# Eight small changes of order in a one-core kernel that runs two transformer blocks: first load, statistics of x, a bank, a rounding step, folds, and the last store

## Time and profile before

| | |
|---|---|
| median of 3 runs | 1286.98 us (1286.67 to 1288.11) |
| the profiled execution | 1287.98 us, its span 1286.2 us |
| TensorE busy | 1246.5 us, 97% |
| weight loads | 1096.5 us, 85% |
| VectorE | 852.2 us, 66% |
| ScalarE | 581.1 us, 45% |
| GpSimd | 101.8 us, 8% |
| transfers | 219.27 MB, 170 GB/s over the span |

### The profile page before, as it was taken

One profiled execution on the slowest core, in us unless ns is written; L12 is line 12 of the kernel. 1 busy time (PEld: TensorE's weight loads), 2 busy tenths in 40 slices (PEclk: granted clock), 3 DMA queues, 4 the chain that ended last, 5 costly groups with the idle time before them and its releaser, 6 DMA issues.

```text
span 1286.2 us, 19279 instructions
## 1 busy us (share of the span) xinstructions
PE 1246.5 (97%) x7697; PEld 1096.5 (85%) x7697; DVE 852.2 (66%) x1327; ACT 581.1 (45%) x926; POOL 101.8 (8%) x101
## 2 busy tenths in 40 slices
PE   6999999999899999999999999999999999999997
PEld 6987999987788888887787798888788997999986
DVE  5885888796697777753424884357886676555544
ACT  7655545444632222222324662246445745544533
POOL 2030001100000000000100400001330000000000
PEclk9999999999999999999999999999999999999999
DMA  8444577775376578863342363334223554555562
GB/s 329 148 140 144 194 246 248 232 243 173 132 223 194 193 233 292 290 221 111 99 137 76 121 183 99 98 99 132 83 85 112 182 180 131 187 185 186 181 196 82
DMA packets 59465, 219.27 MB, mean 170 GB/s; under 512 B 6685, under 2 KB 6721, under 8 KB 58609
## 3 DMA queue, kind: packets, MB, share of 16 engines
q1 hardware_dynamic: 56736, 205.55, 49.7%
q0 software_dynamic: 2352, 11.76, 2.6%
q10 hardware_dynamic: 288, 0.75, 0.2%
HBM read 216.95 MB, written 1.07 MB: 170 GB/s over the span
## 4 chain that ended last, share of the span: by engine, by line
PE 84%; DVE 7%; ACT 5%; issue 2%; DMA 1%; POOL 0%; DVEq 0%; SPq 0%; ACTq 0%; POOLq 0%
PE ps L2088 18%; PE ps L2090 18%; PE ps L2089 18%; PE ps L2136 3%; PE ps L2138 3%; PE ps L2137 3%; PE ps L2147 3%; PE ps L2149 3%; PE ps L2148 3%; ACT hi L693 2%; DVE lo L1291 2%; PE ps L2124 1%; PE ps L2125 1%; PE ps L2126 1%; PE ps L2616 1%
## 5 line engine op out<-in xcount | busy, mean ns | idle before, releaser
L1291 DVE TENSOR_TENSOR lo<-raw,hi 128x1024 fp32r<-128x1024 f32 x315 | 390.6, 1241 | 297.0 <-ACT hi L693 296.7
L2088 PE MATMUL ps<-nh,hi 128*128 128x256 f32 (+1 forms) x1776 | 552.7, 311 | 5.5 <-DVE lo L1291 3.3
L2089 PE MATMUL ps<-nh,lo 128*128 128x256 f32 (+1 forms) x1776 | 545.0, 307 | 0.0
L2090 PE MATMUL ps<-nl,hi 128*128 128x256 f32 (+1 forms) x1776 | 544.9, 307 | 0.0
L693 ACT ACTIVATE hi<-raw 128x1024 fp32r<-128x1024 f32 x315 | 332.3, 1056 | 437.8 <-PE ps L2090 246.7
L2088 PEld LDWEIGHTS ps<-nh,hi 128*128 128x128 f32 x1776 | 340.0, 191 | 36.1 <-issue 15.8
L2089 PEld LDWEIGHTS ps<-nh,lo 128*128 128x128 f32 x1776 | 340.1, 191 | 16.4 <-issue 1.0
L2090 PEld LDWEIGHTS ps<-nl,hi 128*128 128x128 f32 x1776 | 339.9, 191 | 15.2
L707 ACT ACTIVATE sg<-ps 128x256 f32<-128x256 f32 (+1 forms) x66 | 30.1, 455 | 132.8 <-PE ps L2090 132.8
L1278 DVE SCALAR_TENSOR_TENSOR raw<-raw,cvec 128x1024 f32<-128x1024 f32 x72 | 86.8, 1222 | 1.4
L2136 PE MATMUL ps<-hi,H 128*128 128x512 f32 x176 | 70.1, 398 | 4.2 <-DVE lo L1291 3.6
(11 more groups left out here) (372 smaller groups left out, 1316.2 us busy)
## 6 DMA issues: line engine op xcount, KB each, us to landing
raw<-in_up SPq DMA_DIRECT2D x132, 512.0 KB, 3.8
raw<-in_in SPq DMA_DIRECT2D x86, 512.0 KB, 3.6
raw<-in_w_ada SPq DMA_DIRECT2D x72, 512.0 KB, 4.5
raw<-in_down SPq DMA_DIRECT2D x66, 512.0 KB, 3.7
raw<-in_out SPq DMA_DIRECT2D x8, 512.0 KB, 4.0
raw<-in_hy_out SPq DMA_DIRECT2D x8, 512.0 KB, 3.9
raw<-in_da_out SPq DMA_DIRECT2D x8, 512.0 KB, 3.9
raw<-in_o SPq DMA_DIRECT2D x8, 512.0 KB, 3.6
```

Of the source, the lines that this page charges most:

```text
L1291: dve.tensor_tensor(lo[:, h, 0:w], raw[:, r, 0:w], hi[:, h, 0:w].bitcast(F32), ALU.subtract).then_inc(lo_done, 1)
L2088: mm(o, hi[:, h, wk], x_hi, start=first, stop=False)
L2089: mm(o, lo[:, h, wk], x_hi, start=False, stop=False)
L2090: return mm(o, hi[:, h, wk], x_lo, start=False, stop=last)
```

## The change

1. **First load:** at the start only `par[:, 0:8]` is loaded. The other 595 columns and `con` are issued by ScalarE's queue after `nh` of k = 3. Whoever uses the rest of `par` first waits for it (`par_landed` 32).
2. **Sums of x** on TensorE after slab 2 instead of slab 1.
3. **xdt** before `seg` 8 to 11 on VectorE.
4. **A turn's bank:** `turn_values(1)` uses bank 4 and waits for `o1_lo` 1 (VectorE has read bank 4) instead of `pool_lo` 2; `turn_values(2)` waits for `pool_lo` 2.
5. **Rounding** of context column k at slab k + 11 instead of k + 10 on ScalarE.
6. **Folds** wait until TensorE is through the first slab of `k2`.
7. **rows2:** row 3 is added after the first diagonal.
8. **Last store:** the last 512 columns are added and stored in two halves of 256; the last store is issued by ScalarE.

```diff
-    "x": dict(final1=4, post2=8, rows2=4, rows3=4),
+    "x": dict(final1=4, post2=8, rows2=4, rows3=5),
+VALUES_IN = (5, 4, 5)
+OUT_PARTS = ((0, 0, 512), (0, 512, 512), (1, 0, 512), (1, 512, 256), (1, 768, 256))
-            for b in range(4):
-                tt, w = b // 2, slice(b % 2 * 512, b % 2 * 512 + 512)
+            for b, (tt, at, n) in enumerate(OUT_PARTS[:-1]):
+                w = slice(at, at + n)
                 sp.wait_ge(sem("x"), since("x", "rows3") + b + 1)
                 sp.dma_start(out[:, tt, w], xtok[:, tt, w]).then_inc(sem("out_landed"), 16)
-            sp.wait_ge(sem("out_landed"), 64)
+            sp.wait_ge(sem("out_landed"), 80)
+            pool.wait_ge(slab_used, st["k2"][0].s + 1)
             pool.wait_ge(sem("kf_copied"), 6)
-            act.dma_start(par[:, :], d["params"]).then_inc(sem("par_landed"), 16)
-            act.dma_start(con[:, :], d["consts"]).then_inc(sem("con_landed"), 16)
+            act.dma_start(par[:, 0:KD], d["params"][:, 0:KD]).then_inc(sem("par_landed"), 16)
...
                 if k == 3:
+                    act.dma_start(par[:, KD:NPAR], d["params"][:, KD:NPAR]).then_inc(sem("par_landed"), 16)
+                    act.dma_start(con[:, :], d["consts"]).then_inc(sem("con_landed"), 16)
...
             act.wait_ge(sem("con_landed"), 16)
+            act.wait_ge(sem("par_landed"), 32)
             prime(0, ACT.Sqrt)
...
-                               ps[:, 5, 0:256].rearrange("p (a n) -> p a n", a=2), ACT.Copy)\
+                               ps[:, VALUES_IN[t], 0:256].rearrange("p (a n) -> p a n", a=2), ACT.Copy)\
...
-                if 10 <= x.j < 18:
-                    rounded("pre2c", xgc, x.j - 10, c_)
+                if 11 <= x.j < 19:
+                    rounded("pre2c", xgc, x.j - 11, c_)
...
+            tt, at, n = OUT_PARTS[-1]
+            act.wait_ge(sem("x"), since("x", "rows3") + len(OUT_PARTS))
+            act.dma_start(out[:, tt, at:at + n], xtok[:, tt, at:at + n]).then_inc(sem("out_landed"), 16)
...
             after(1)
+            dve.wait_ge(sem("par_landed"), 32)
...
                 if p == 10:
-                    segments(8, 12)
                     dve.wait_ge(sem("ssd_made"), 1)
...
+                    segments(8, 12)
                 if p == 11:
...
-            added_row("rows2", 3, 1, free[3])
             row_inverse("rows2", 2, ROOT + 2, INV + 2)
             diagonal("rows2", 3, 0, INV + 2)
+            added_row("rows2", 3, 1, free[3])
...
-                for b in (2 * tt, 2 * tt + 1):
+                for b in (2 * tt, 2 * tt + 1)[:2 - tt]:
                     added_row("rows3", b, 4 + tt, free[b])
+            for at in (512, 768):
+                w = slice(at, at + 256)
+                dve.wait_ge(bank_free[3], free[3])
+                dve.scalar_tensor_tensor(xr[:, 1, w], yg[:, 1, w], small[:, INV + 5:INV + 6], xr[:, 1, w],
+                                         ALU.mult, ALU.add).then_inc(sem("x"), 1)
...
-                    o = pe.transpose(ps[:, 5, tt * P:tt * P + P],
+                    o = pe.transpose(ps[:, VALUES_IN[t], tt * P:tt * P + P],
...
-                if p == 1:
+                if p == 2:
                     gathered("mix1", rinv[:, :], SUM1)
...
                 if p == 20:
-                    pe.wait_ge(sem("pool_lo"), 2)
+                    pe.wait_ge(sem("o1_lo"), 1)
                     turn_values(1)
...
-            pe.wait_ge(sem("vtok_copied"), 2)
+            pe.wait_ge(sem("pool_lo"), 2)
             turn_values(2)
```

## The result

The changed kernel takes 1278.44 us (median of 4 runs, 1278.41 to 1278.81), the kernel before beside it 1286.83 (1286.16 to 1288.11): ratio 0.9923, 95% interval 0.991 to 0.9937. That is 8.4 us faster where 14.7 were forecast, and 2 us above the top of the range. The profiled execution took 1278.81 us, its span 1277.0, where the one before took 1287.98 and 1286.2; the sum is checked against these two, a difference of 9.2.

The account below looks back on a forecast made before the run. The prediction took TensorE to bound the kernel, busy 97% of the span, with pauses and clock falls to gain. Its terms summed to -14.7 from 1287.98 us, less 1.0 for the median: 1272.3 us, range 1269.5 to 1276.5.

Parts of the forecast that it names:

- First load: At the start: fewer bytes ahead of x and slab 0 bring the first product earlier, later `con` costs nothing; -0.9 us.
- Sums of x: Early slabs: slab 2 fills the 2.56 us pause, but most returns as pauses, some 2 us before slab 6; -0.8 us.
- xdt: TensorE's 1.2 us wait for `xdt` ends, but its next products wait for `xw`; -0.4 us.
- A turn's bank: At the turn of V: the 2.71 us pause and its low clock go, slab 21 waits some 0.4; -3.5 us.
- Rounding: In `down1`: roundings leave ScalarE's circle and follow 2.72 apart, not 3.15; the 2.2 us pause goes; -5.4 us.
- Folds: In `mixed`: GpSimd's folds slow VectorE's splits; moved into `k2` they cost TensorE nothing; -3.2 us.
- rows2: Row 3's addition, 0.74 us, no longer stands before the first diagonal; -0.2 us.
- Last store: At the end: half the bytes in the last store and a shorter VectorE addition before it; -0.3 us.
- rival 1: Clock falls in a pause the change makes before slab 6, or stays low at the turn: +1.3 us; chance 0.16.
- Rival 4: At the start: first load gives nothing because issues or a late `con` eat it: +1.8 us; chance 0.06.
- rival 2: Folds aren't the cause in `mixed`, or cost as much in `k2`: +3.2 us; chance 0.07.
- Rival 5: TensorE, without its rests, gets a lower mean clock; at 0.98 the time is 1297.2 us; chance 0.02.

Follow-up runs that it names:

- con_wait_later: Changed kernel with TensorE's wait for `con` moved from behind slab 0 to ahead of the sums of x, after slab 2: 1274.92 us.
- sums_as_before: Changed kernel with the sums of x after slab 1 again, first load still split: 1275.56 us.
- filled_pause: con_wait_later with 16 more products of no use on TensorE after slab 5, in the pause before slab 6: 1273.72 us.
- wait_and_sums_at_1: Changed kernel with both the wait for `con` and the sums of x behind slab 1, first load still split: 1274.55 us.
- old_load: Changed kernel with `par` and `con` loaded whole at the start again, sums still after slab 2: 1276.48 us.
- old_start: Changed kernel with both the first load and the sums of x as before, the six other edits kept: 1275.81 us.
- no_round_no_folds: Changed kernel with the rounding of the context and the folds put back where they were before: 1288.56 us.
- start_edits_only: Kernel before with only the split first load, the sums after slab 2 and the last store in halves: 1292.49 us, ratio 1.0027.
- two_more_banks: con_wait_later with slabs 6 and 7 of `in1` in banks 7 and 5, so TensorE waits for an earlier `take_in`: 1274.52 us.
- banks_and_block_later: two_more_banks with the small products that wait for `dtok_copied`, and VectorE's copies of their results, one slab later: 1272.23 us.

## Why the prediction was wrong

Each part's measure is how much later or earlier the same product comes in the two traces behind it than ahead of it.

| part | forecast | measured | by |
|---|---|---|---|
| first load, sums, xdt | -0.9, -0.8, -0.4 | +2.5 | the product behind the wait for `vtok` at 80.94 for 78.45 |
| turn's bank | -3.5 | -3.3 | +2.5 before it, -0.8 behind it |
| rounding | -5.4 | -5.2 | -0.8, then -6.0 |
| folds | -3.2 | -3.1 | +0.2 at the start of `mixed`, -3.3 through it |
| rows2 | -0.2 | -0.1 | -9.1, then -9.3 |
| last store | -0.3 | +0.1 | last product to end 6.06, then 6.13 |
| sum | -14.7 | -9.2 | |

- **The step that failed** is in *First load*: "`con` ... next needed behind the squares of x, several us after their issue ... so I cost them at nothing." The kernel says otherwise of TensorE: it waits for `con` behind slab 0, though it uses it only at the sums. That wait came up at 13.0, seven us after the issue, and lasted to 15.36. The step named ScalarE's table switch as the first in line and left out TensorE's own wait, which the list of places above names. Also wrong was to judge the landing by `par`'s 5.6 us at the very start: 275 KB took 6.4 and `con` 9.3. con_wait_later removes this one wait; slab 6 is 3.7 us earlier and the time 3.5 less. The gain that the term counted was there: the first product came 1.2 us earlier, not 0.9. (`par` has 558 columns, not 603, and with 275 KB of it 724.5 KB are moved, not 728; the 1.8 stays.)
- **How much of the miss this is.** The first three terms were to give 2.1 us and cost 2.5: 4.6 of the 5.5 us missed. The other five terms are short by 1.0 together.
- **Sums of x.** The end of the mechanism was right: VectorE's line sets slab 6, and the largest pause goes there (2.19, forecast some 2). But the prediction let the reciprocal stand behind the splits of slabs 3 and 4 whatever TensorE does, with a root "that is ready earlier". In the changed kernel the root is later, and VectorE waits 1.87 us for it at 24.27: with `con` late, the sums' move costs 2.9 us (sums_as_before) where 0.8 were to be gained. In con_wait_later slab 6 is 2.5 before its place in the trace of before (31.98 for 34.45), more than the 1.7 forecast. But the clock fell behind that pause, rival 1, which I gave 0.16: +1.4 from slab 6 to the product behind it (filled_pause gives back 1.2). With `con` out of the way load and sums together are worth -1.1 at that product (36.51 for 37.56), where -1.7 was forecast and -0.4 with rival 1. The sums' part of it is nothing (con_wait_later against wait_and_sums_at_1) or a small loss (0.3 in the traces of old_load and old_start).
- **Rival 4**, a late `con`, was priced at the loss of the 0.9, 1.8 with the other bound. It cost twice that, 3.5: the wait of 2.4 was handed on to the root and VectorE's splits, and the clock fell behind it.
- **xdt.** -0.2: old_start is 0.15 late at the product ahead of it (52.87 for 52.72) and 0.06 early behind the wait for `vtok` (78.39 for 78.45). The first product behind `xdt` gained 1.0, and the products that need `xw`, with a wait of 0.6, took 0.8 of it back, more than the forecast allowed.
- **Turn, rounding, folds** came within 0.2 of their terms, by the mechanisms given: slab 21 done 3.3 earlier, 2.72 between roundings, 2.88 between the slabs of `mixed`. no_round_no_folds brings back both sets of waits. That the splits' slowness comes from GpSimd's folds is supported by the three means above, and it follows them into `k2`, where it costs TensorE nothing; with the folds back in `mixed`, in no_round_no_folds, the mean over 716 to 733 us is 1839 ns again. That rival 2's other cause, work of ScalarE in `mixed`, adds something, wasn't tested alone; it can't be much, as no wait for `lo` is left there.
- **Last store.** The forecast took 0.3 us for half the bytes off the landing: 128 KB land in 2.6 us and 256 KB in 2.5. The Trainium skill (DMA: Bandwidth & Descriptors, Anatomy of one DMA — SWDGE (gpsimd) path) gives a transfer that GpSimd issues a fixed part of about 2 us and a part by size. These stores were issued by SP and ScalarE, and their landings show no part by size. VectorE's two halves take 0.14 us more than the whole did (0.88 for 0.74).
- **Rival 5** is out: the mean clock is 0.997, and was 0.996 before.

## What to carry to other kernels

Before a load is put later, list every wait for it on every engine, in the order of the queues, and take each at the place where it stands and not where the data are used; a wait that stands too early is harmless only as long as the load is. When a pause is filled, find what the next engine in the line still sets: here the pause came back before slab 6 at nearly the same length, and only more banks and a later block of small products removed it. Cost a pause of two us with the low clock behind it as a case of its own, for it comes in some executions and not in others. And where two edits lie in the same stretch, don't add their terms before you have asked what the one does with the other's delay: load and sums lost 2 to 3 us only together.

## What the runs showed of the chip

A pause of the same length drops the clock in one execution and not in the next. Before slab 6, 2.18 or 2.19 us of pause were followed by 0.50 in the changed kernel, con_wait_later and old_load (4.4 to 4.6 us to the product behind slab 6), and by 1.00 in start_edits_only and no_round_no_folds (3.2). In `down1` 2.17 us were followed by 1.00 in the kernel before and by 0.50 in those two. The windows, first start_edits_only behind both of its pauses, then the kernel before behind the one in `down1`:

```profile
38.00:39.00 1.00, 1.00 (x10) 1.00 (x10) 0.96 (x3) 0.72 (x1) 0.00 (x0) 1.00 0.09 33
329.00:330.00 1.00, 1.00 (x3) 0.75 (x3) 1.00 (x2) 0.00 (x0) 0.00 (x0) 0.50 0.95 336
```

```profile
326.00:327.00 1.00, 1.00 (x6) 0.79 (x5) 1.00 (x2) 0.00 (x0) 0.00 (x0) 1.00 0.86 319
```

In the traces, pauses of 1.7 us (two_more_banks before its small products, the kernel before at rows2) didn't drop it; one of 2.1 (wait_and_sums_at_1) did, and so did all of 2.4 us and more. A fall cost 1.4 to 1.6 us (slab 1 and slab 6 of the changed kernel, `down1`).

The kernel before seems to spread for the same reason. Its 33 runs beside the ten kernels fall into three groups, each with its mean clock: 1285.85 to 1286.83 us at 0.998 or 0.999, 1288.00 to 1289.38 at 0.996, 1290.76 to 1291.29 at 0.994. Its profiled execution, 1287.98 us with two falls, has 0.996. So it is likely that the fastest runs had fewer falls, though the pauses of 2.56 and 2.71 us are in the kernel, and the slowest more; which fell isn't shown, as only one run has a trace. A thousandth or two of the mean clock alone proves nothing: the runs of banks_and_block_later, in whose trace the clock is low only behind the last product, take 1272.17 to 1272.40 us at 0.998 and at 1.000. Nor does a pause of this length by itself make a kernel's runs spread: old_load has one of 2.19, and its four lie within 0.16 us.
